# Two feed-forward layers: the first two weight pieces multiplied by token halves of 128 columns

## Chip, cores and metric

The kernel runs on one core of a Trainium2 chip. The metric is device time in microseconds (us) of one execution. Five engines work side by side: TensorE (PE; its weight loads are shown as PEld), VectorE (DVE), ScalarE (ACT), GpSimd (POOL) and SyncE (SP, which issues most transfers).

## What is computed

The program computes a hybrid attention layer with a 32-expert feed-forward part on 256 tokens of width 1024, and behind it a block of two layers. The change lies in that second block:

```python
for layer in range(DEPTH_2):
    h = rmsnorm(x, norm_mix_g[layer])
    ...
    x = x + y
    h = rmsnorm(x, norm_ffn_g[layer])
    x = x + swiglu_ffn(h, ffn_w_gate[layer], ffn_w_up[layer], ffn_w_down[layer])
return rmsnorm(x, final_g)
```

`swiglu_ffn` is `(silu(h @ w_gate) * (h @ w_up)) @ w_down`, with 256 rows in `h`, 1024 columns, and 2816 hidden columns. Layer 0 mixes tokens by Fourier and convolution heads ahead of it, layer 1 by a pooling mixer.

## The kernel before

Products of the feed-forward layers are made to nearly float32 precision out of three matmuls on rounded float32 (fp32r). Each weight matrix is cut into pieces of 128 hidden columns by 1024 rows. ScalarE rounds a piece to `wh` (L2527, function `hi`), VectorE subtracts that from the original to get `wl` (L1637, function `lo`), and the helper `mm3` (L573 to L576) multiplies high by high (L574), high by low (L575) and low by high (L576). The activations are held turned (features on partitions, tokens on columns), split in the same way into `HTH` and `HTL`, each [128, 8 groups `k` of features, 256 tokens]. So a piece takes 8 values of `k` times 3 = 24 matmuls, each with a weight load of 128x128 and 256 moving columns. Pieces `n` = 0 and 1 are the first two halves of the first gate unit, n = 2 and 3 those of the first up unit. Four pairs of buffers `wh`, `wl` go round: `hi` of piece n waits until piece n-4 is "used".

Each engine runs its own list of instructions strictly in the order in which the code writes it; semaphore counts with names (`done((...))`) tie the lists together. What leads into a feed-forward layer runs for two token halves `i` = 0 and 1 of 128 tokens:

1. PE ends the mixer's output matmuls (L1476 in layer 0, L1620 in layer 1) and VectorE adds them to the residual `X` (`add`, L2295), in two halves of 512 columns.
2. ScalarE sums the squares (`squares`, L2889) and takes the root (L2894), VectorE takes the reciprocal (L2299, in `scale`).
3. VectorE scales the half into `XN` (`normed`, L2310, two instructions).
4. PE turns it: 8 transposes of 128x128 (`turned`, L1393) into PSUM.
5. ScalarE writes the rounded `HTH` (`high`, L2907), VectorE the rest `HTL` (`low`, L2318), 8 instructions each of 128 columns. They go in groups `q`: half 0 has two groups of four values of `k`, half 1 has four groups of two.

On PE the order around it is: `turned(st, 0)`, then in `ffn` `turned(st, 1)`, then piece after piece over all 256 tokens; before the matmuls of piece 0 for k = 0, 2, 4, 6 `turned_ready` (L1396) waits for `HTL` of both halves:

```python
pe.wait_ge(*done(("HTL", l, 0, k // 4)))
pe.wait_ge(*done(("HTL", l, 1, k // 2)))
```

In layer 0 two of the mixer's last matmuls are kept behind `turned("ffn0", 0)`. In layer 1 ScalarE does `squares` of both halves ahead of `high`, and VectorE does `normed` of both halves ahead of `low`; `lo` of piece 1 stands behind all of `low`. POOL scales the pooling map (L3227 and L3232) long before layer 1 and then waits for the last mixer matmul.

The gate and up products of a step j fill two PSUM banks; behind them come the sigmoid, two multiplications, and the split into `FTH` and `FTL`; and after 44 pieces the 22 pieces of the down matrix. SyncE fetches weights into a ring of slots; `emptied` names the step that must be done before a slot is filled anew, for a gate unit the `lo` of its second piece.

Of the kernel before, what the change touches and what calls it, by code (L numbers as in the profile page):

```python
# [7 lines left out]
F32 = mybir.dt.float32  # L8
# [193 lines left out]
def build(nc, I, out, counts, counting):  # L202
    with ExitStack() as ctx:
# [23 lines left out]
        def done(name):  # L227

            if counting and name not in counts:
                return sig["pe_ada"].sem, 1  # L230
            key, n = counts[name]
            return sig[key].sem, n
# [316 lines left out]
        def emptied(name):  # L549

            kind = name[0]
            if kind in ("in", "out", "abc", "abr", "gate", "up", "down"):
                st, n = {
                    "in": lambda: ("in", AT_PIECE[name[1], 2 * name[2] + 1]),
                    "out": lambda: ("out", 2 * OUT_KK.index(name[1]) + 1),
                    "abc": lambda: ("ab", 2 * AB.index(name[1]) + 1),
                    "abr": lambda: ("ab", 9 + 2 * name[1]),
                    "gate": lambda: (f"ffn{name[1]}", 4 * name[2] + 1),
                    "up": lambda: (f"ffn{name[1]}", 4 * name[2] + 3),
                    "down": lambda: (f"ffn{name[1]}", 2 * NFF + 2 * name[2] + 1),  # L560
                }[kind]()
                return [(st, "lo", n)]
            if kind == "w1":
                return [("w1", name[1], name[2] + wide(name)), ("w1b", name[1], (0, 1, 2, 2)[name[2] // 2])]
            if kind == "w2":
                return [("w2", name[1], name[2] + wide(name)), ("w2b", name[1])]
            if kind == "dft":
                return [("width", 3)]
            if kind == "outab" and name[1] == 2:
                return [("outab", 3)]  # L570
            return [name]
# [15 lines left out]
        def _(pe):  # L587
# [801 lines left out]
            def turned(l, i):  # L1389
                for q, b, ks in turns(l, i):  # L1390
                    pe.wait_ge(*done(("normed", l, i, 0 if q == 0 else 1)))
                    for k in ks:
                        t = pe.transpose(turn_at(b, k, l, i), XN[:, i, k * 128:(k + 1) * 128], ident)  # L1393
                    t.then_inc(*P.tick(("n turned", l, i, q)))

            def turned_ready(l, k):  # L1396

                pe.wait_ge(*done(("HTL", l, 0, k // 4)))
                pe.wait_ge(*done(("HTL", l, 1, k // 2)))
# [149 lines left out]

            def ffn(l, then):  # L1550
                st, gu = f"ffn{l}", 4 - 4 * l
                turned(st, 1)
                for j in range(NFF // 2):
                    bg, bu = [(gu, gu + 1), (gu + 2, gu + 3)][j % 2]
                    for bank in (bg, bu):
                        for m in range(2):
                            n = 4 * j + 2 * (bank == bu) + m
                            _, hi, lo, _, _ = piece(st, n)
                            pe.wait_ge(*done((st, "lo", n)))
                            if bank == bg and m == 0 and j >= 2:  # L1560
                                pe.wait_ge(*done((st, "gated", j - 2)))
                            for k in range(8):
                                if n == 0 and k % 2 == 0:
                                    turned_ready(st, k)
                                t = mm3(pe, PS[:, bank, m * 256:(m + 1) * 256], hi[:, k, :], lo[:, k, :], HTH[:, k, :],
                                        HTL[:, k, :], k == 0, k == 7)
                            t.then_inc(*P.tick((st, "used", n)))

                def down(k, i, ns):
                    _, hi, lo, _, _ = piece(st, 2 * NFF + k)  # L1570
                    pe.wait_ge(*done((st, "lo", 2 * NFF + k)))
                    return mm3(pe, PS[:, 4 - gu + 2 * i + ns, :], FTH[:, k, i * 128:(i + 1) * 128],
                               FTL[:, k, i * 128:(i + 1) * 128], hi[:, ns * 512:(ns + 1) * 512],
                               lo[:, ns * 512:(ns + 1) * 512], k == 0, k == NFF - 1)

                for k in range(NFF - 4):
                    if k % 2 == 0:
                        pe.wait_ge(*done((st, "f", k // 2)))
                    for i, ns in LAST:
                        t = down(k, i, ns)  # L1580
                    t.then_inc(*P.tick((st, "used", 2 * NFF + k)))
                pe.wait_ge(*done((st, "f", NFF // 2 - 1)))
                for ks in ((NFF - 4, NFF - 3), (NFF - 2, NFF - 1)):
                    for ns in range(2):
                        for k in ks:
                            t = down(k, 0, ns)
                        if k == NFF - 1:
                            t.then_inc(*P.tick((st, "down", 0, ns)))
                for ns in range(2):
                    if ns:  # L1590
                        then()
                    for k in range(NFF - 4, NFF):
                        t = down(k, 1, ns)
                    t.then_inc(*P.tick((st, "down", 1, ns)))
# [36 lines left out]
        def _(dve):  # L1631
            V = sig["dve_ada"]

            def lo(st, n):
                src, h, l, _, _ = piece(st, n)
                dve.wait_ge(*done((st, "hi", n)))
                dve.tensor_tensor(l, src, h.bitcast(F32), ALU.subtract).then_inc(*V.tick((st, "lo", n)))  # L1637
# [664 lines left out]
            def base(l, i):  # L2302

                dve.wait_ge(*done(("sq", l, i)))
                dve.tensor_scalar(rb[i], sqs[i][0], 1.0 / 1024, 1e-6, ALU.mult, ALU.add).then_inc(*V.tick(("rb", l, i)))

            def normed(l, i):
                scale(l, i)
                for n, c in enumerate((slice(0, 256 << (1 - i)), slice(256 << (1 - i), 1024))):
                    dve.tensor_scalar(XN[:, i, c], X[:, i, c], rr[i], None, ALU.mult).then_inc(*V.tick(("normed", l, i, n)))  # L2310

            def low(l, i, qs):
                for q, b, ks in turns(l, i):
                    if q in qs:
                        dve.wait_ge(*done(("HTH", l, i, q)))
                        for k in ks:
                            c = slice(128 * i, 128 * i + 128)
                            t = dve.scalar_tensor_tensor(out=HTL[:, k, c], in0=turn_at(b, k, l, i),  # L2318
                                                         scalar=gk(GAIN[l])(k), in1=HTH[:, k, c].bitcast(F32),
                                                         op0=ALU.mult, op1=ALU.subtract)  # L2320
                        t.then_inc(*V.tick(("HTL", l, i, q)))
# [165 lines left out]
            normed("ffn1", 0)  # L2487
            add(1, 1, PS[:, 3, :], ("pmap",), "x5")
            base("ffn1", 1)
            normed("ffn1", 1)  # L2490
            low("ffn1", 0, [0])
            low("ffn1", 1, [0, 1])
            low("ffn1", 0, [1])
            low("ffn1", 1, [2, 3])
            lo("ffn1", 1)

            V = sig["dve_ffn1"]
            ffn(1, 2)
# [20 lines left out]
        def _(act):  # L2519
# [378 lines left out]
            def both(l, name, i):  # L2898
                for _ in squares(l, name, i):
                    pass  # L2900

            def high(l, i, qs):
                for q, b, ks in turns(l, i):
                    if q in qs:
                        act.wait_ge(*done(("n turned", l, i, q)))
                        for k in ks:
                            t = act.activation(HTH[:, k, 128 * i:128 * i + 128], turn_at(b, k, l, i), ACT.Copy,  # L2907
                                               scale=gk(GAIN[l])(k))
                        t.then_inc(*S.tick(("HTH", l, i, q)))
# [165 lines left out]
                               ACT.Copy).then_inc(*S.tick(("pooled", g)))  # L3075
            hi("ffn1", 1)
            both("ffn1", "x5", 0)
            both("ffn1", "x5", 1)
            high("ffn1", 0, [0])
            high("ffn1", 1, [0, 1])  # L3080
            high("ffn1", 0, [1])
            high("ffn1", 1, [2, 3])

            S = sig["act_ffn1"]
            ffn(1, 2)
# [10 lines left out]
        def _(pool):  # L3096
# [133 lines left out]
            for g in range(4):  # L3230
                for c in range(2):
                    pool.tensor_tensor(pm[:, g, c, :], pm[:, g, c, :], PSC[:, 256 * g:256 * g + 256], ALU.mult).then_inc(  # L3232
                        *G.tick("map scaled"))
            pool.wait_ge(*done(("pmap",)))
            small("final", FG, I["final_g_2"].rearrange("(a n) -> a n", a=1).to_broadcast([128, 1024]))

# [153 lines left out]
```

## Time and profile before

| what | us |
|---|---|
| median of three runs | 1626.15 (1625.92 to 1627.06) |
| the profiled execution's own time | 1627.0 |
| its span, first to last instruction | 1625.2 |
| PE busy | 1525.5 (94%) |
| VectorE busy | 670.8 (41%) |
| ScalarE busy | 456.1 (28%) |
| POOL busy | 111.4 (7%) |
| layer 0: first and 49th feed-forward matmul start | 1222.54 and 1229.05 |
| layer 1: first and 49th feed-forward matmul start | 1430.15 and 1438.50 |

The 49th matmul of a layer is the first of piece 2, so the stretch before it is that of pieces 0 and 1. The granted clock of TensorE is 1.00 at 2.4 GHz and 0.50 at 1.2 GHz. A matmul's busy time in the trace includes its way through the array, so neighbours overlap; the pace of a stream is read from the distance between starts.

### The profile page before, as it was taken

How to read it: one execution, taken by the hardware profiler on the slowest of the kernel's cores; microseconds unless marked ns; L12 is line 12 of the kernel's file. 1: busy time of each engine (PE TensorE's matmuls, PEld its weight loads, DVE VectorE, ACT ScalarE, POOL GpSimd, SP SyncE). 2: the span in 40 equal slices, each digit the busy share in tenths (PEclk: the TensorE clock that was granted, in tenths of full speed). 3: DMA queues.
4: the chain of work that ended last, by engine and by line, in shares of the span. 5: the costliest groups of instructions: out<-in, count | busy, mean ns of one | idle time of the engine just before them, and what ended most of it. 6: DMA issues, size and time to landing. Idle time of an engine off the chain costs nothing. (4 is left out here: it accounts for less than half of the span.)

```text
span 1625.2 us, 21576 instructions
## 1 busy us (share of the span) xinstructions
PE 1525.5 (94%) x8585; PEld 872.0 (54%) x8585; DVE 670.8 (41%) x970; ACT 456.1 (28%) x760; POOL 111.4 (7%) x124
## 2 busy tenths in 40 slices
PE   7999999999999998999998989887999999999998
PEld 4888534333333323333332323223849998799986
DVE  4676632323323222232222222224866655465654
ACT  3565311011101110111110101003765444354443
POOL 4132200000000000000000000000620003100000
PEclk9999999999999999999999989999999999999999
DMA  9977999999999999999999999999537555465530
GB/s 348 383 217 279 379 385 427 425 405 410 426 426 426 425 426 428 426 426 425 427 425 427 427 425 426 426 423 337 174 104 246 182 183 187 137 205 183 181 104 27
DMA packets 113394, 534.27 MB, mean 329 GB/s; under 512 B 7013, under 2 KB 70140, under 8 KB 87376
## 3 DMA queue, kind: packets, MB, share of 16 engines
q1 hardware_dynamic: 111232, 529.97, 82.2%
q8 instruction: 121, 1.98, 0.5%
q0 software_dynamic: 2000, 1.98, 0.4%
q14 instruction: 41, 0.34, 0.1%
HBM read 530.87 MB, written 1.05 MB: 327 GB/s over the span
## 5 line engine op out<-in xcount | busy, mean ns | idle before, releaser
L1019 PE MATMUL ps<-ring,arena 128*64 128x512 f32 x2024 | 485.2, 604 | 17.4 <-DMA ring<-in_w_mlp 15.3
L1019 PEld LDWEIGHTS ps<-ring,arena 128*64 128x64 f32 x2024 | 130.1, 136 | 252.6 <-issue 209.1
L1037 PE MATMUL ps<-ring,arena 128*64 128x512 f32 x1024 | 231.8, 598 | 19.4 <-DMA ring<-in_w_mlp 13.4
L1637 DVE TENSOR_TENSOR wl<-ring,wh 128x1024 fp32r<-128x1024 f32 x132 | 162.1, 1232 | 135.8 <-ACT wh L2527 135.8
L574 PE MATMUL ps<-hth,wh 128*128 128x256 f32 x704 | 201.1, 286 | 0.7 <-DVE htl L2318 0.7
L575 PE MATMUL ps<-htl,wh 128*128 128x256 f32 x704 | 198.9, 282 | 0.0
L576 PE MATMUL ps<-hth,wl 128*128 128x256 f32 x704 | 198.2, 282 | 0.0
L2118 DVE TENSOR_TENSOR arena<-ps,arena 128x1024 f32<-128x1024 f32 x68 | 83.3, 1224 | 249.4 <-PE ps L1044 244.0
L2527 ACT ACTIVATE wh<-ring 128x1024 fp32r<-128x1024 f32 x132 | 139.2, 1059 | 148.8 <-PE ps L576 148.7
L1037 PEld LDWEIGHTS ps<-ring,arena 128*64 128x64 f32 x1024 | 76.9, 137 | 166.8 <-issue 136.7
L2143 DVE TENSOR_TENSOR arena<-ps,arena 128x512 f32<-128x512 f32 x34 | 23.5, 691 | 337.5 <-PE ps L1037 334.4
L575 PEld LDWEIGHTS ps<-htl,wh 128*128 128x128 f32 x704 | 135.9, 193 | 0.0
L576 PEld LDWEIGHTS ps<-hth,wl 128*128 128x128 f32 x704 | 134.7, 191 | 0.0
L574 PEld LDWEIGHTS ps<-hth,wh 128*128 128x128 f32 x704 | 133.7, 190 | 1.2 <-issue 1.0
L2795 ACT ACTIVATE arena<-arena 128x512 f32<-128x512 f32 (+1 forms) x33 | 20.4, 617 | 303.3 <-DVE arena L2131 303.3
L2816 ACT ACTIVATE obh<-arena 128x512 fp32r<-128x512 f32 x30 | 18.9, 630 | 294.0 <-DVE arena L2143 294.0
L574 PE MATMUL ps<-wh,fth 128*128 128x512 f32 x176 | 69.7, 396 | 0.0
L575 PE MATMUL ps<-wl,fth 128*128 128x512 f32 x176 | 69.6, 395 | 0.0
L576 PE MATMUL ps<-wh,ftl 128*128 128x512 f32 x176 | 69.4, 395 | 0.0
L3211 POOL MEMSET arena<- 128x1144 f32 x1 | 1.1, 1063 | 951.0 <-DVE htl L2318 951.0
L2776 ACT ACTIVATE arena<-ps,arena 128x256 f32<-128x256 f32 x60 | 30.6, 559 | 117.9 <-PE ps L990 112.9
L574 PE MATMUL ps<-wp,ht 128*128 128x384 f32 (+1 forms) x128 | 46.2, 361 | 2.9 <-DVE wp L1637 2.7
(456 smaller groups left out, 1853.8 us busy)
## 6 DMA issues: line engine op xcount, KB each, us to landing
ring<-in_w_mlp SPq DMA_DIRECT2D x187, 2048.0 KB, 27.8
ring<-in_ffn_w_gate SPq DMA_DIRECT2D x22, 1024.0 KB, 5.4
ring<-in_ffn_w_up SPq DMA_DIRECT2D x22, 1024.0 KB, 5.4
ring<-in_ffn_w_down SPq DMA_DIRECT2D x22, 1024.0 KB, 4.9
ring<-in_w_ada SPq DMA_DIRECT2D x16, 1024.0 KB, 9.7
ring<-in_w_ada SPq DMA_DIRECT2D x16, 512.0 KB, 11.4
ring<-in_w_mlp SPq DMA_DIRECT2D x8, 1024.0 KB, 34.4
ring<-in_w_in SPq DMA_DIRECT2D x10, 768.0 KB, 12.6
```

The lines of the kernel that those rows point to most:

```text
L574: pe.matmul(o, lh, rh, start=first, stop=False)
L575: pe.matmul(o, lh, rl, start=False, stop=False)
L576: return pe.matmul(o, ll, rh, start=False, stop=last)
L1019: t = pe.matmul(PS[64 * g:64 * g + 64, HB[hb][ns], :], x[:, k8, :], u[:, f:f + 512], start=False, stop=k8 == 7)
L1037: t = pe.matmul(PS[64 * g:64 * g + 64, 3, :], a4[:, kc, 64 * kg:64 * kg + 64], u[:, c, g * 512:(g + 1) * 512], start=k8 == 0, stop=k8 == 7)
L1637: dve.tensor_tensor(l, src, h.bitcast(F32), ALU.subtract).then_inc(*V.tick((st, "lo", n)))
L2118: dve.tensor_tensor(x, PS[:, b:b + 2, :], x, ALU.add).then_inc(*tick(name))
L2143: dve.tensor_tensor(OBF, PS[:, bank, :], G2R, ALU.mult).then_inc(*tick(n_f))
L2527: act.activation(h, src, ACT.Copy).then_inc(*S.tick((st, "hi", n)))
L2776: act.activation(XGT[b % 2][:, k, :], PS[:, bank, (k % 2) * 256:(k % 2) * 256 + 256], ACT.Identity, scale=a2[:, k:k + 1], bias=sh2[:, k:k ...
L2795: act.activation(SIG[:, 0:n], GLU[:, 0:n], ACT.Sigmoid, scale=1.702).then_inc(*Q.tick(name))
L2816: act.activation(OBH[0], OBF, ACT.Copy).then_inc(*SM.same())
```

## The change

In both layers pieces 0 and 1 are multiplied over 128 tokens at a time. PE takes token half 0 for k = 0 to 3 of piece 0 and of piece 1 (24 matmuls of 128 moving columns), then turns half 1, then takes half 0 for k = 4 to 7 of both pieces (24), then half 1 of piece 0 and of piece 1 (48). From piece 2 on nothing changes. In layer 1 ScalarE and VectorE do their parts in another order, and POOL does the subtraction `lo` of piece 1, which waits for `hi` of that piece; SyncE's wait for the slot of layer 1's first gate unit names both pieces, since two engines now read it.

```diff
@@ def emptied(name)
+            if name == ("gate", 1, 0):
+                return [("ffn1", "lo", 0), ("ffn1", "lo", 1)]
@@ block.tensor, def ffn(l, then)
                 st, gu = f"ffn{l}", 4 - 4 * l
-                turned(st, 1)
+
+                def token_half(n, i, k):
+                    _, hi, lo, _, _ = piece(st, n)
+                    c, o = slice(128 * i, 128 * i + 128), n * 256 + 128 * i
+                    return mm3(pe, PS[:, gu, o:o + 128], hi[:, k, :], lo[:, k, :], HTH[:, k, c], HTL[:, k, c],
+                               (n, i, k) == (0, 0, 0), (n, i, k) == (1, 1, 7))
+
+                for q in range(2):
+                    pe.wait_ge(*done(("HTL", st, 0, q)))
+                    for n in range(2):
+                        pe.wait_ge(*done((st, "lo", n)))
+                        for k in range(4 * q, 4 * q + 4):
+                            token_half(n, 0, k)
+                    if q == 0:
+                        turned(st, 1)
+                for n in range(2):
+                    for k in range(8):
+                        if k % 2 == 0:
+                            pe.wait_ge(*done(("HTL", st, 1, k // 2)))
+                        t = token_half(n, 1, k)
+                    t.then_inc(*P.tick((st, "used", n)))
                 for j in range(NFF // 2):
                     bg, bu = [(gu, gu + 1), (gu + 2, gu + 3)][j % 2]
-                    for bank in (bg, bu):
+                    for bank in (bg, bu) if j else (bu,):
@@
                             for k in range(8):
-                                if n == 0 and k % 2 == 0:
-                                    turned_ready(st, k)
@@ block.vector
             base("ffn1", 1)
+            low("ffn1", 0, [0])
             normed("ffn1", 1)
-            low("ffn1", 0, [0])
-            low("ffn1", 1, [0, 1])
             low("ffn1", 0, [1])
-            low("ffn1", 1, [2, 3])
-            lo("ffn1", 1)
+            low("ffn1", 1, range(4))
@@ block.scalar
             both("ffn1", "x5", 0)
-            both("ffn1", "x5", 1)
+            part = squares("ffn1", "x5", 1)
+            next(part)
             high("ffn1", 0, [0])
-            high("ffn1", 1, [0, 1])
+            next(part)
             high("ffn1", 0, [1])
-            high("ffn1", 1, [2, 3])
+            high("ffn1", 1, range(4))
@@ block.gpsimd
+            src, high, low, _, _ = piece("ffn1", 1)
+            pool.wait_ge(*done(("ffn1", "hi", 1)))
+            pool.tensor_tensor(low, src, high.bitcast(F32), ALU.subtract).then_inc(*G.tick(("ffn1", "lo", 1)))
```

The change adds lines above these places, so L574 to L576 of before are L576 to L578 of the changed program, L1393 is L1395, L1476 is L1478.

On PE at the start of layer 0's feed-forward part the order before is this (L1393 the transposes; `wh_91` and `wl_92` belong to piece 0):

```order
L1393 MATMUL ps<-arena 128x128 x8
L1476 MATMUL ps<-ring,arena 128x512 x2
L1393 MATMUL ps<-arena 128x128 x8
L574 MATMUL ps<-hth,wh_91 128x256
L575 MATMUL ps<-htl,wh_91 128x256
L576 MATMUL ps<-hth,wl_92 128x256
L574 MATMUL ps<-hth,wh_91 128x256
```

In the changed program the same place reads as follows (L1395 the transposes; `wh_93` and `wl_94` belong to piece 1; 18 more matmuls of 128 columns stand where the rows are left out):

```order
L1478 MATMUL ps<-ring,arena 128x512 x2
L576 MATMUL ps<-hth,wh_91 128x128
L577 MATMUL ps<-htl,wh_91 128x128
L578 MATMUL ps<-hth,wl_92 128x128
...
L576 MATMUL ps<-hth,wh_93 128x128
L577 MATMUL ps<-htl,wh_93 128x128
L578 MATMUL ps<-hth,wl_94 128x128
L1395 MATMUL ps<-arena 128x128 x8
L576 MATMUL ps<-hth,wh_91 128x128
```

The second turning has moved from ahead of all feed-forward matmuls to behind the first 24 of them, and these have 128 columns. In layer 1 the two turnings, which stood together, are parted in the same way.

On VectorE the order ahead of layer 1's feed-forward part is this before (L2295 `add`, L2310 `normed`, L2318 `low`, L1637 `lo`):

```order
L2295 TENSOR_TENSOR arena<-arena,ps 128x512
L2305 TENSOR_SCALAR arena<-arena 128x1
L2299 RECIPROCAL arena<-arena 128x1
L2310 TENSOR_SCALAR arena<-arena 128x256
L2310 TENSOR_SCALAR arena<-arena 128x768
L2318 SCALAR_TENSOR_TENSOR htl<-ps,arena,hth 128x128 x16
L1637 TENSOR_TENSOR wl_94<-ring,wh_93 128x1024
```

and this in the changed program (L2338 is `low`, L2330 `normed`, L2319 the reciprocal):

```order
L2315 TENSOR_TENSOR arena<-arena,ps 128x512
L2325 TENSOR_SCALAR arena<-arena 128x1
L2338 SCALAR_TENSOR_TENSOR htl<-ps,arena,hth 128x128 x4
L2319 RECIPROCAL arena<-arena 128x1
L2330 TENSOR_SCALAR arena<-arena 128x256
L2330 TENSOR_SCALAR arena<-arena 128x768
L2338 SCALAR_TENSOR_TENSOR htl<-ps,arena,hth 128x128 x12
L1657 TENSOR_TENSOR wl_96<-ring,wh_95 128x1024
```

Four instructions of `low` stand ahead of the second half's reciprocal and scaling, and piece 1's subtraction has gone to POOL.

## Rows read from the trace of the kernel before

**Rows 1.** The page: busy time of each engine, and granted clock in 40 slices.

```profile
PE 1525.5 (94%) x8585; PEld 872.0 (54%) x8585; DVE 670.8 (41%) x970; ACT 456.1 (28%) x760; POOL 111.4 (7%) x124
...
PEclk9999999999999999999999989999999999999999
```

**Rows 2.** Stretches: stretch, length, busy us (count) of each engine, granted clock, DMA share, GB/s.

```profile
1218.00:1220.60 2.60, 0.00 (x0) 0.00 (x0) 2.49 (x10) 1.18 (x4) 0.59 (x1) 1.00 0.55 126
1220.60:1222.50 1.90, 1.84 (x8) 1.34 (x8) 1.09 (x3) 1.26 (x5) 0.00 (x0) 0.57 1.12 396
1230.00:1400.00 170.00, 170.00 (x1224) 159.94 (x1223) 96.15 (x93) 76.34 (x84) 18.45 (x16) 1.00 0.59 192
...
1427.90:1430.10 2.20, 1.43 (x8) 0.84 (x8) 2.20 (x8) 2.11 (x9) 0.00 (x0) 0.77 1.10 388
1430.10:1435.00 4.90, 4.84 (x23) 4.88 (x24) 4.78 (x13) 3.43 (x8) 0.00 (x0) 0.50 0.27 103
```

**Rows 3.** Timeline into layer 0: start, us, engine, instruction, [idle before, releaser].

```profile
1215.10 1.04 PE L1393 MATMUL ps<-arena 128*128 128x128 f32 x8
...
1217.17 1.13 DVE L2318 SCALAR_TENSOR_TENSOR htl<-ps,arena,hth 128x128 fp32r<-128x128 f32 x4 [0.87 <-ACT hth L2907]
...
1220.20 0.88 DVE L2310 TENSOR_SCALAR arena<-arena 128x256 f32<-128x256 f32 x2
...
1220.61 2.07 PE L1393 MATMUL ps<-arena 128*128 128x128 f32 x8 [2.75 <-DVE arena L2310]
...
1222.54 0.55 PE L574 MATMUL ps<-hth,wh 128*128 128x256 f32 x1
...
1224.46 0.28 PE L574 MATMUL ps<-hth,wh 128*128 128x256 f32 x1
...
1229.05 0.28 PE L574 MATMUL ps<-hth,wh 128*128 128x256 f32 x1
```

**Rows 4.** Timeline into layer 1.

```profile
1418.66 1.05 ACT L2527 ACTIVATE wh<-ring 128x1024 fp32r<-128x1024 f32 x1
...
1425.34 1.04 PE L1393 MATMUL ps<-arena 128*128 128x128 f32 x8
...
1427.95 1.53 PE L1393 MATMUL ps<-arena 128*128 128x128 f32 x8 [1.57 <-DVE arena L2310]
...
1430.15 0.55 PE L574 MATMUL ps<-hth,wh 128*128 128x256 f32 x1 [0.68 <-DVE htl L2318]
...
1435.84 0.33 PE L576 MATMUL ps<-hth,wl 128*128 128x256 f32 x1
...
1438.50 0.28 PE L574 MATMUL ps<-hth,wh 128*128 128x256 f32 x1
```

**Rows 5.** Timeline of PE: float32 matmuls of 128 and of 64 moving columns.

```profile
73.39 2.84 PE L719 MATMUL ps<-arena 128*128 128x128 f32 x24
...
122.10 0.39 PE L743 MATMUL ps<-arena 128*128 128x64 f32 x2
122.33 0.39 PE L744 MATMUL ps<-arena 128*128 128x64 f32 x2
```

**Rows 6.** Instructions that read or write hth, and L745's: duration ns minimum/median/maximum.

```profile
L574 PEld LDWEIGHTS ps<-hth,wh x704: 186/187/330, 1222.5 to 1557.4; 128*128 128x128 f32 x176
...
L745 PEld LDWEIGHTS ps<-arena x24: 192/192/193, 121.8 to 140.7; 128*128 128x128 f32 x24
```

**Rows 7.** Timeline of PE: fp32r matmuls of 512 moving columns, in layer 0's down part.

```profile
1411.15 0.40 PE L575 MATMUL ps<-wl,fth 128*128 128x512 f32 x1
...
1412.55 0.40 PE L575 MATMUL ps<-wl,fth 128*128 128x512 f32 x1
```

**Rows 8.** Timeline of PE into the first mixer (1130 to 1136 us).

```profile
1130.23 3.67 PE L1393 MATMUL ps<-arena 128*128 128x128 f32 x16 [3.84 <-DVE arena L2310]
...
1135.58 0.28 PE L576 MATMUL ps<-hth,wm 128*128 128x256 f32 x1
```

**Rows 9.** POOL's timeline ahead of layer 1.

```profile
1377.91 8.47 POOL L3232 TENSOR_TENSOR ring<-ring,arena 128x256 f32<-128x256 f32 x8
```

## The prediction

> **What bounds the kernel now.** I read the page first. TensorE is busy for 94% of the span, no other engine for half of it, and the granted clock is nearly always full [rows 1]. The stretches show the same for the feed-forward layers: from 1230 to 1400 us TensorE is busy in every microsecond and moves no more than the matmuls need, while VectorE, ScalarE and the transfers have time to spare [rows 2]. So whatever the change wins or loses before piece 2 of a layer goes straight to the end of the program. The two places to look at are the ways into the layers, and for those I read the timelines.
>
> Layer 0: TensorE turns half 0 at 1215.10, VectorE has finished the first group of its `HTL` at 1217.17 + 1.13 = 1218.30, but TensorE does nothing for 2.6 us [rows 2], waits for the second half's scaling, turns it from 1220.61, and begins piece 0 at 1222.54. Piece 2 begins at 1229.05 [rows 3]. The idle time costs twice: in the stretch 1220.60 to 1222.50 the clock is granted at 0.57 on average, that is mostly at 1.2 GHz [rows 2], and only from about 1224.3 on are the matmuls at full pace: 39 from 1224.46 to 1229.05, 0.118 us apart [rows 3]. Layer 1: half 0 is turned from 1425.34, half 1 from 1427.95, piece 0 begins at 1430.15; the clock is at 0.50 from 1430.10 to 1435.00 [rows 2], 27 matmuls from 1430.15 to 1435.84 start 0.211 apart, then the clock is full, and piece 2 begins at 1438.50 [rows 4].
>
> **The price that decides: a matmul of 128 columns.** The change makes 96 matmuls of 128 columns in each layer out of 48 of 256. The columns are the same, the weight loads are doubled. No row shows an fp32r matmul with 128 moving columns, so I bound it.
> - From below: 512 columns start 0.233 apart (six from 1411.15 to 1412.55) [rows 7], 256 columns 0.118 [rows 3]. That is 0.00045 us a column, and 128 columns would take 0.0605 us, if the weight load never showed.
> - From above, as one instruction: not more than 256 columns take, 0.118 us.
> - The nearest rows: float32 matmuls with the same 128x128 weights. 24 with 128 columns take 2.84 us with the last one's 0.28 in it, so 23 steps of 0.111. And pairs with only 64 columns take 122.33 - 122.10 = 0.23, so 0.111 to 0.115 each again [rows 5]. Half the columns, the same pace: what sets it is not the columns but the weight load. The load of an fp32r matmul lasts 187 ns in the trace, that of those float32 ones 192 [rows 6], so I take it to be the same load.
>
> I take 0.111 us, from these rows. Ninety-six then cost 10.66 us, where 48 of 256 columns cost 5.66 at full clock: the halves save nothing on the array and double the loads. The Trainium skill has two rules here, and they disagree. In "TensorE: Matmul & The Clock Gate", section "Back-to-back issue gap", the isolated gap is columns/2.4 + 2.5 ns, which is 56 ns for 128 columns and would make the change a gain; its section "LDWEIGHTS (loading the stationary operand)" gives weight columns/1.2 ns, 107 ns for 128, and [rows 5] agree with that one.
>
> **Layer 0, step by step.** The first 24 matmuls can start when the first group of `HTL` is there, at 1218.30, say 1218.4 (4.1 us sooner than now). The clock is still granted in full from 1218.00 to 1220.60 [rows 2], although TensorE rests there; with matmuls in that stretch I take it to stay so. 24 x 0.111 = 2.66, to 1221.06. The second half's scaling runs from 1220.20 to 1221.08 [rows 3], so the transposes, which now stand behind the 24, find it ready and begin 0.45 us later than now; at full clock 8 take 0.89 (the first eight took 1.04 including the last one's way through [rows 3]), to 1221.95. While ScalarE and VectorE make the second half's `HTH` and `HTL`, TensorE has the next 24 matmuls of half 0, to 1224.6. By then these eight copies and subtractions, 2.4 us long now, are done, so nothing waits. 72 x 0.111 = 7.99, to 1229.94. Against 1229.05: **+0.9 us**.
>
> **Layer 1.** From the turning's start to the first group of `HTL` layer 0 takes 1218.30 - 1215.10 = 3.2 us [rows 3]; ScalarE and VectorE now do this group first here too, so it is ready at 1425.34 + 3.2 = 1428.5, and TensorE starts at 1428.6, 1.55 us sooner. TensorE idles for 2.2 us ahead of that. The clock fell at about 1429.1 in the present run after 1.6 us of idle (0.77 over 1427.90 to 1430.10 is 1.2 us at full and 1.0 at half [rows 2]), and I expect it to fall there again. It then stays low for 3.4 us, as in layer 0 (from about 1220.9, read off 0.57 over its stretch, to 1224.3), or twice that, as here now (1429.1 to 1435.9). I take the short one, since matmuls now run through without a gap. At half clock a matmul with 128x128 weights starts every 0.213 to 0.22 us (transposes: 16 in 3.67 [rows 8]). So 4.5 matmuls by 1429.1, 16 by 1432.5, 3.5 to 1432.9. The scaling of half 1, which now lets the transposes go at 1427.95 [rows 4], slides behind one group of copies and subtractions, by about 1.1 us. That costs nothing, because the transposes must wait for TensorE until 1432.9 anyway: this is what is late next. Transposes to 1433.8, 72 matmuls to 1441.8. Against 1438.50: **+3.3 us**.
>
> **The rest.** `lo` of piece 1 on POOL: 8 of 256 columns take 8.47 us [rows 9], so 1024 take 4.2 us, from the end of `hi` of piece 1 at 1418.66 + 1.05 = 1419.7 [rows 4] to 1424; it is wanted at 1429. Cover: 5 us. If it slowed VectorE in that time, some tenths would be lost in adds that TensorE's mixer matmuls hide. VectorE is freed of 1.2 us. ScalarE and VectorE prepare pieces 2 and 3 (four instructions, about 4.5 us in a chain) behind the second half's groups, in layer 1 by about 1439; they are wanted at 1441.8. SyncE's wait for the slot of the first gate unit now has two names, and the later one is met some 10 us sooner than now: nothing. PSUM: the bank written early is free, its adds are long done.
>
> **Sum.** +0.9 and +3.3 are +4.2 us on a span of 1625.2. The profiled execution took 1627.0, 0.85 above the median; the difference is the same for both, so 1626.15 + 4.2 = **1630.3 us**. A measurement can tell about 0.2%, 3.25 us, from no change: this is just beyond it.
>
> **Rivals.**
> 1. *No low clock in layer 1.* With matmuls from 1428.6 the clock may not fall at all. Then layer 1 loses 1.65 instead of 3.3, together +2.5: 1628.7, no change to measure. Against it: 2.2 us of idle stand ahead. Chance 0.17.
> 2. *Faster: the weight load hides under 128 columns.* At the lower bound of 0.0605 us TensorE reaches the transposes of layer 0 before 1220.61, waits for the scaling, ends them at 1221.8 and 72 matmuls at 1226.2: -2.9. Layer 1: 24 to 1431.0 (0.12 at low clock), transposes to 1432.7, 72 to 1437.1: -1.4. Together -4.3: 1621.9. It decides at the price of a matmul: 192 of them at 0.088 us are even, below 0.070 the change is faster by over 0.2%. For it: the turning of half 1 is truly hidden. Against it: 64 columns went no faster than 128 [rows 5]. The 56 ns of the Trainium skill's "Back-to-back issue gap" would be this case; the same section has 81 ns for a sustained stream of loads and matmuls, which would give about -1 us; no row shows either. Chance 0.11.
> 3. *Short fp32r matmuls go at the plain float32 rate.* A plain float32 product shows as two matmul records of 0.111 us each [rows 5]. Were 128 columns of fp32r treated so, 192 more records make +21.3: 1651.6. For it: no fp32r matmul below 256 columns is in the kernel. Chance 0.06.
> 4. *The short matmuls hold the clock low.* If a stream that is half weight loads doesn't bring the clock back, 72 matmuls and more at 0.213 give +10.8 and +13.3: 1650.3. Against it: before the first mixer the clock came back at 1135.5 after 16 transposes of 128 columns, a gap and five matmuls [rows 8]. Chance 0.06.
>
> **How the numbers follow.** The forecast has 0.60: of that 0.50 lies above +3.25 and 0.10 below it (a pace of 0.105 already takes 1.2 us off). Rival 1 gives 0.17 to no change; rival 2 has 0.09 for faster and 0.02 for no change; rivals 3 and 4 give 0.12 to slower. Sum: faster 0.09, no change 0.29, slower 0.62. Range: on the upper side a short low clock in layer 0 too (+1.6), the long one in layer 1 (+1.6) and 0.118 for the pace (+1.3) reach 1635; on the lower side it takes in rival 1 and the upper half of rival 2, to 1623.5. Rivals 3 and 4 and the rest of 2 are left out, about 0.2.
>
> **What would show it.** Right: 128-column matmuls 0.111 us apart at full clock; the first at about 3.2 us behind the first turning; no idle time between them, and transposes of half 1 waiting for TensorE, not for VectorE; piece 2 at about +0.9 us in layer 0 and +4.2 in layer 1 against now. Wrong: starts 0.06 to 0.09 apart, or 0.22 at full clock; a clock that stays at 0.50 beyond four microseconds; TensorE waiting for the second half's `HTL`, or for piece 1 from POOL.

## The result, and the profile after

The changed kernel takes 1632.97 us in the median of six runs (1631.65 to 1635.96), the kernel before 1626.04 (1624.36 to 1627.06). The ratio is 1.0045 with a 95% interval of 1.0034 to 1.0056: 6.9 us slower, where 4.2 were forecast. The profiled execution took 1635.96 us, the slowest of the six, with a span of 1634.2.

The page of the changed kernel, lines that answer to [rows 1]:

```profile
PE 1538.0 (94%) x8681; PEld 881.2 (54%) x8681; DVE 669.9 (41%) x969; ACT 456.1 (28%) x760; POOL 113.4 (7%) x125
...
PEclk9999999999999999999999999998999999999999
```

TensorE has 96 more matmuls (8681 against 8585) and is busy 12.5 us longer. Where the time went is read by stretches, each from one start to another in the same trace, so that a later beginning doesn't count. The timeline of PE into layer 0 (start, us, engine, instruction, [idle before, releaser]), against [rows 3]:

```profile
1216.68 1.04 PE L1395 MATMUL ps<-arena 128*128 128x128 f32 x8
...
1219.92 0.33 PE L576 MATMUL ps<-hth,wh 128*128 128x128 f32 x1 [0.49 <-DVE htl L2338]
...
1222.66 1.06 PE L1395 MATMUL ps<-arena 128*128 128x128 f32 x8
1223.47 0.31 PE L576 MATMUL ps<-hth,wh 128*128 128x128 f32 x1
1223.62 0.28 PE L577 MATMUL ps<-htl,wh 128*128 128x128 f32 x1
1223.73 0.27 PE L578 MATMUL ps<-hth,wl 128*128 128x128 f32 x1
...
1231.55 0.33 PE L576 MATMUL ps<-hth,wh 128*128 128x256 f32 x1
```

The half matmuls start 0.11 us apart; 72 of them and the step to the next take 1231.55 - 1223.47 = 8.08 us, 0.112 each. The transposes wait for TensorE and for nobody else. From the first turning to piece 2: 14.87 us, before 13.95.

Into layer 1, against [rows 4], all engines:

```profile
1429.54 1.04 PE L1395 MATMUL ps<-arena 128*128 128x128 f32 x8
...
1432.53 0.33 PE L576 MATMUL ps<-hth,wh 128*128 128x128 f32 x1 [1.95 <-DVE htl L2338]
...
1433.14 0.40 PE L578 MATMUL ps<-hth,wl 128*128 128x128 f32 x1
1433.33 0.42 PE L576 MATMUL ps<-hth,wh 128*128 128x128 f32 x1
1433.55 0.41 PE L577 MATMUL ps<-htl,wh 128*128 128x128 f32 x1
...
1437.18 1.93 PE L1395 MATMUL ps<-arena 128*128 128x128 f32 x8
1437.86 2.17 ACT L2925 ACTIVATE hth<-ps,arena 128x128 fp32r<-128x128 f32 x8 [4.58 <-PE ps L1395]
...
1439.86 0.34 PE L578 MATMUL ps<-hth,wl 128*128 128x128 f32 x1
1440.04 0.28 PE L576 MATMUL ps<-hth,wh 128*128 128x128 f32 x1
...
1447.40 0.34 PE L576 MATMUL ps<-hth,wh 128*128 128x256 f32 x1
```

The clock falls within the half matmuls, at 1433.15, from then on they start 0.21 us apart, and it is full again only at 1439.97, 6.8 us later. ScalarE waits 4.58 us for the second turning, which is queued behind the 24 halves. From the first turning to piece 2: 17.86 us, before 13.16.

The stretches of the changed kernel (stretch, length, busy us and count of PE, PEld, DVE, ACT, POOL, granted clock, DMA share, GB/s), against [rows 2]:

```profile
1219.90:1231.50 11.60, 11.57 (x104) 11.58 (x105) 8.39 (x19) 6.15 (x14) 0.42 (x1) 1.00 0.97 316
1415.00:1418.00 3.00, 1.40 (x7) 0.79 (x5) 0.75 (x2) 0.80 (x3) 0.00 (x0) 1.00 0.00 0
1418.00:1421.00 3.00, 2.00 (x11) 2.00 (x12) 2.11 (x4) 1.75 (x3) 0.00 (x0) 0.75 0.00 0
1429.50:1432.50 3.00, 1.07 (x9) 0.79 (x7) 2.09 (x8) 2.29 (x9) 0.62 (x1) 1.00 0.42 122
1432.50:1440.00 7.50, 7.47 (x38) 7.47 (x39) 3.44 (x13) 2.92 (x13) 0.00 (x0) 0.54 0.88 303
1440.00:1447.40 7.40, 7.40 (x68) 7.40 (x68) 4.27 (x6) 2.98 (x4) 0.00 (x0) 1.00 0.37 117
```

Layer 0 has a full clock throughout, layer 1 a low one for 6.8 of the 7.5 us. And there is a third place that was not in the forecast: the pooling stage, where the clock is low too, from 1419.5 to 1422.9. The second group of pooling matmuls is that place's row in both timelines, first before, then changed:

```profile
1416.47 2.12 PE L1604 MATMUL ps<-ring,arena 128*128 128x136 f32 x16 [2.60 <-DVE ring L2469]
```

```profile
1419.00 3.56 PE L1624 MATMUL ps<-ring,arena 128*128 128x136 f32 x16 [2.60 <-DVE ring L2489]
```

The same 2.60 us of rest ahead of it, the same work, 1.4 us longer. The sum of the two profiled spans, 1634.2 - 1625.2 = 9.0 us:

| stretch | before | changed | difference |
|---|---|---|---|
| start to layer 0's first turning | 1215.10 | 1216.68 | +1.58 |
| layer 0, first turning to piece 2 | 13.95 | 14.87 | +0.92 |
| piece 2 to layer 1's first turning | 196.29 | 197.99 | +1.70 |
| layer 1, first turning to piece 2 | 13.16 | 17.86 | +4.70 |
| piece 2 to the end | 186.70 | 186.80 | +0.10 |

The first line lies ahead of everything that the change touches. All traces below differ there (the first turning of layer 0 is at 1212.4 to 1216.7). The timed runs of one kernel scatter by about as much; that it is for the same reason is not shown, since only one or two runs of each kernel have a trace.

### The profile page after: what moved, and what is told of

Its sections match the earlier page's. It is cut to its first block and busy times, and to the rows that moved or that the text cites. A ratio compares the mean times of both kernels' runs of the same rounds, so it can differ in the third digit from the quotient of the medians.

```text
span 1634.2 us, 21765 instructions
## 1 busy us (share of the span) xinstructions
PE 1538.0 (94%) x8681; PEld 881.2 (54%) x8681; DVE 669.9 (41%) x969; ACT 456.1 (28%) x760; POOL 113.4 (7%) x125
## 5 line engine op out<-in xcount | busy, mean ns | idle before, releaser
L576 PE MATMUL ps<-hth,wh 128*128 128x256 f32 (+1 forms) x736 | 209.2, 284 | 2.4 <-DVE htl L2338 2.4
L577 PE MATMUL ps<-htl,wh 128*128 128x256 f32 (+1 forms) x736 | 207.0, 281 | 0.0
L578 PE MATMUL ps<-hth,wl 128*128 128x256 f32 (+1 forms) x736 | 206.5, 281 | 0.0
L577 PEld LDWEIGHTS ps<-htl,wh 128*128 128x128 f32 x736 | 141.5, 192 | 0.0
L576 PEld LDWEIGHTS ps<-hth,wh 128*128 128x128 f32 x736 | 139.4, 189 | 3.5 <-DVE htl L2338 3.5
L578 PEld LDWEIGHTS ps<-hth,wl 128*128 128x128 f32 x736 | 140.5, 191 | 0.0
L576 PE MATMUL ps<-wh,fth 128*128 128x512 f32 x176 | 69.7, 396 | 0.0
L578 PE MATMUL ps<-wh,ftl 128*128 128x512 f32 x176 | 69.4, 394 | 0.0
L576 PE MATMUL ps<-wp,ht 128*128 128x384 f32 (+1 forms) x128 | 46.1, 360 | 2.9 <-DVE wp L1657 2.7
```

Of the source, the lines that this page charges most:

```text
L576: pe.matmul(o, lh, rh, start=first, stop=False)
L577: pe.matmul(o, lh, rl, start=False, stop=False)
L578: return pe.matmul(o, ll, rh, start=False, stop=last)
```

## The experiments

The verdicts rest on two measures: the ratio of the timed runs, which resolves 1 to 2 us here, and the same two stretches in each trace, which resolve a tenth within one execution but move with the clock from one execution to the next. "L0" and "L1" are the times from a layer's first turning to piece 2; before they are 13.95 and 13.16, changed 14.87 and 17.86.

### One layer at a time

For layer 0 alone, the halves stand under a condition, and layer 1 runs as before:

```diff
-                turned(st, 1)
+                if l == 0:
+                    def token_half(n, i, k):
...
+                else:
+                    turned(st, 1)
```

> Layer 0 in token halves, layer 1 as before. Theory (doubled weight loads against an earlier start, two layers that add up): piece 2 of layer 0 begins 14.9 us behind the first turning instead of 13.95, so +0.9 us in the median, and the way into layer 1 is that of before (13.2 us from turning to piece 2). Rival (the loss sits in layer 0's halves and what they set off later, the clock of the pooling stage among it): +2.5 us or more.

Measured: 1627.62 against 1627.23 us, ratio 1.0001 (0.9990 to 1.0011). L0 14.88, L1 11.72. The +0.93 of layer 0 is that of the changed kernel; the timed runs can't tell it from nothing, but they exclude the rival's +2.5. L1 was expected at 13.2 and came out at 11.72, in code that is that of before: the low clock there varies from one execution to the next.

For layer 1 alone, the condition is turned round, and the orders of the change on ScalarE, VectorE and POOL are kept.

> Layer 1 in token halves with the new order on ScalarE, VectorE and POOL, layer 0 as before. Theory: +4.7 us as in the changed kernel's trace if the low clock lasts 6.7 us, +3.3 if it lasts 3.4; the median between 3.3 and 5. Rival (the loss of the changed kernel is spread): +3 or less.

Measured: 1633.24 us, ratio 1.0036 (1.0023 to 1.0049), 5.9 us by the ratio and above the 3.3 to 5 expected. L0 14.25, L1 24.18. So layer 1 carries the loss, and in the profiled execution, the slowest of the six with 1641.43 us, it was 11 us, not 4.7. L0 is code of before, and 14.25 where the trace of before has 13.95: the low clock there began 0.9 us behind the second turning, at 1222.86, in place of 0.3, and ended at 1226.27. The clock stayed low through all halves (columns as above):

```profile
1433.00:1436.00 3.00, 3.00 (x16) 3.00 (x16) 0.47 (x2) 1.13 (x5) 0.00 (x0) 0.50 1.03 354
1436.00:1440.00 4.00, 4.00 (x21) 4.00 (x21) 3.67 (x9) 2.94 (x7) 0.00 (x0) 0.50 0.04 13
1440.00:1445.00 5.00, 5.00 (x26) 5.00 (x25) 0.38 (x1) 0.00 (x0) 0.00 (x0) 0.50 0.64 208
1445.00:1450.00 5.00, 5.00 (x25) 5.00 (x25) 1.23 (x1) 1.06 (x1) 0.00 (x0) 0.50 0.01 5
```

TensorE is busy in every microsecond and its clock doesn't come back.

### The price of the halves without their place

Both halves are turned first, in the order of before; only pieces 0 and 1 are multiplied as 96 matmuls of 128 columns.

```diff
                 turned(st, 1)
+                for n in range(2):
+                    pe.wait_ge(*done((st, "lo", n)))
+                    for k in range(8):
+                        if n == 0 and k % 2 == 0:
+                            turned_ready(st, k)
+                        for i in range(2):
+                            t = token_half(n, i, k)
+                    t.then_inc(*P.tick((st, "used", n)))
...
```

> Order of before in both layers, all halves turned first; only the 48 matmuls of pieces 0 and 1 are made as 96 of 128 columns. Theory (the weight load sets the pace): 0.111 us apart at full clock, so 96 x 0.111 - 48 x 0.118 = +5.0 us in each layer, +10 in all; at low clock each costs 0.213 like one of 256 columns, so the first 9 and 27 slots hold half the work and the sum is rather +11 to +13. Rival (the 128-column matmul costs half and the loss came from the order): within 1 us of before.

Measured: 1655.7 us, ratio 1.0179 (1.0165 to 1.0193): +28.5 us. L0 27.91, L1 25.34. Both theories miss. The trace of layer 0 shows why (stretch, then the end of the halves in the timeline):

```profile
1222.70:1243.20 20.50, 20.50 (x98) 20.50 (x97) 5.23 (x9) 3.95 (x7) 0.00 (x0) 0.50 0.54 176
```

```profile
1242.77 0.41 PE L575 MATMUL ps<-htl,wh 128*128 128x128 f32 x1
1242.98 0.41 PE L576 MATMUL ps<-hth,wl 128*128 128x128 f32 x1
1243.19 0.52 PE L574 MATMUL ps<-hth,wh 128*128 128x256 f32 x1
...
1245.01 0.38 PE L576 MATMUL ps<-hth,wl 128*128 128x256 f32 x1
1245.22 0.28 PE L574 MATMUL ps<-hth,wh 128*128 128x256 f32 x1
```

All 96 halves, 20.5 us, run at the low clock that the rest ahead of them left. 2.0 us into the matmuls of 256 columns it is full again. Before, the same place was low for 3.4 us. All five timed runs lie at 1653.4 us or above. This is the mechanism of rival 4, for which I had 0.06.

I then formed the theory that a stream of halves doesn't raise a low clock but holds a full one. The same kernel with idle matmuls on TensorE's rests tests it; `fill` is the tool of all runs below with idle matmuls:

```diff
+                def fill(times, cols=256):
+                    _, hi, _, _, _ = piece(st, 0)
+                    pe.wait_ge(*done((st, "lo", 0)))
+                    for _ in range(times):
+                        pe.matmul(PS[:, gu + 1, 0:cols], hi[:, 0, :], hi[:, 0:2, :].rearrange("p k n -> p (k n)")[:, 0:cols],
+                                  start=True, stop=True)
+
+                fill(22 if l == 0 else 12)
                 turned(st, 1)
+                fill(4)
```

> Halves behind both turnings in both layers, as in the run that was 28 us slower, with the same idle matmuls as the run before this one. Theory (a stream of 128-column matmuls does not bring a low clock back, but holds a full one): every half matmul 0.111 us apart at full clock, so 5.0 us a layer more than 48 of 256 columns; in all +7 us against before, +10 against before with idle matmuls. Rival (such a stream lowers the clock by itself): low clock again and +20 or more.

Measured: 1633.52 us, ratio 1.0049 (1.0034 to 1.0063): +6.9 us against before, as expected; against before with idle matmuls (1625.71, below) 7.8 where 10 was expected. L0 18.14, L1 15.57. All halves at full clock:

```profile
1221.70:1232.50 10.80, 10.79 (x98) 10.79 (x97) 5.04 (x9) 3.76 (x7) 0.00 (x0) 1.00 1.03 343
```

### The changed kernel with its rest in layer 1 filled

```diff
+                fill(0 if l == 0 else 15)
                 for q in range(2):
                     pe.wait_ge(*done(("HTL", st, 0, q)))
```

> The changed kernel with 15 more matmuls of 256 columns into an unused bank on TensorE in layer 1, between the first turning and the wait for its HTL. Theory (two thirds of layer 1's loss is the low clock that the 2 us of rest bring): the clock stays full there, 24 halves in 2.7 us, and the kernel is 3 us faster than the changed one (from +6.9 to about +3.9 against before); the first half matmul starts at the same place or at most 0.2 us later. Rival (the clock is not set by that rest): no change against the changed kernel, low clock in the same place.

Measured: 1629.68 us, ratio 1.0016 (1.0007 to 1.0026): against the kernel before beside it (1627.23) a loss of 2.5 us in place of 6.9. L0 14.88, L1 14.61 in place of 17.86. The first half starts 2.99 us behind the turning, as without idle matmuls. Timeline and stretches:

```profile
1427.35 1.04 PE L1395 MATMUL ps<-arena 128*128 128x128 f32 x8
1428.14 2.04 PE L1565 MATMUL ps<-wh 128*128 128x256 f32 x15
1430.34 0.33 PE L576 MATMUL ps<-hth,wh 128*128 128x128 f32 x1 [0.16 <-DVE htl L2346]
```

```profile
1427.30:1430.30 3.00, 2.88 (x24) 2.63 (x23) 2.10 (x8) 2.28 (x9) 0.62 (x1) 1.00 0.51 121
1430.30:1442.00 11.70, 11.66 (x105) 11.66 (x105) 7.73 (x18) 5.93 (x15) 0.00 (x0) 1.00 0.70 231
```

So the low clock was 3.25 us of layer 1's 4.70. The other 1.45 are against a layer that had 6.8 us of low clock itself. Against the kernel before with its rests filled (L0 13.18, L1 11.61, below) the change costs 1.70 us in layer 0 and 3.00 in layer 1 at full clock, and the traces split that in two:

| us | layer 0 | layer 1 |
|---|---|---|
| price of the halves at full clock: late halves with idle matmuls, less before with them | 18.14 - 13.18 = +4.96 | 15.57 - 11.61 = +3.96 |
| the early start (in layer 1 with the new orders): this run, less late halves with idle matmuls | 14.88 - 18.14 = -3.26 | 14.61 - 15.57 = -0.96 |
| together, at full clock | +1.70 | +3.00 |
| lost to the low clock before | 13.95 - 13.18 = 0.77 | 13.16 - 11.61 = 1.55 |
| lost to it in the changed kernel's profile | 0 | 17.86 - 14.61 = 3.25 |

With these, 1.70 - 0.77 = +0.93 and 3.00 + 3.25 - 1.55 = +4.70 are the two differences of the profiles. The price is 1 us lower in layer 1, where 256 columns at full clock have to stop for an `HTL` (0.61 us, shown below) and the halves don't. The idle time that the change removes was worth less than the doubled matmuls even where no clock fell.

### The changed kernel once more

> The changed kernel once more, for a second trace. Theory (layer 1's loss depends on where the low clock meets the half matmuls): layer 0 again 14.9 us from turning to piece 2; layer 1 one of three values, about 14.8 (no low clock), 17.9 (low for the first halves) or 24 (low through all halves, as in the run with layer 1 alone). Rival (layer 1's loss is fixed): 17.9 again.

Measured: a single run of 1641.94 us. L0 14.87, L1 23.99. The stretch of the halves in layer 1:

```profile
1430.50:1451.50 21.00, 21.00 (x105) 21.00 (x105) 7.68 (x18) 5.87 (x14) 0.00 (x0) 0.53 0.47 158
```

The same program, the same rest (1.96 us of waiting against 1.95), and the clock low for 7 us in one execution, and in the other from about the 12th half to the last and beyond. The two are not equally common: this stream of layer 1 was run 13 times (six runs of the changed kernel, this one, six with layer 1 alone), and two lie above 1641 us, this one and the profiled one of the run with layer 1 alone. The other eleven took 1631.5 to 1636.0 us.

### The kernel before with its rests filled

> The kernel before, with idle matmuls of 256 columns (into an unused bank) on TensorE while it rests: layer 0, 22 ahead of the second turning and 4 behind it; layer 1, 12 and 4. Nothing else is moved. Theory (half of what the changed kernel does well is only the clock): the clock is full at both ways in, layer 0 from turning to piece 2 takes 13.0 us instead of 13.95 and layer 1 10.4 instead of 11.7 to 13.2, so 2 to 3.5 us faster than before. Rival (the clock falls for other reasons, or the idle matmuls push the real ones back): no gain, or a loss of up to 1 us.

Measured: 1625.71 against 1626.58 us, ratio 0.9993 (0.9983 to 1.0003). L0 13.18, L1 11.61, at full clock. The traces show the 2.3 us (0.77 and 1.55) that were expected at the lower end, although L1 was expected at 10.4; the timed runs can't tell them from nothing, and layer 1 of before has 11.7 to 13.2 anyway.

> The kernel before with the same number of idle matmuls, of 64 moving columns each, weights 128x128 as ever. Theory (the weight load sets the pace): they too start 0.111 us apart, like those of 128 columns, so they fill the rest as well; whether they hold the clock is open. Rival (columns set the pace, 128 columns cost 0.111 for another reason): 0.06 apart or less.

The edit is the 64 as second argument of `fill`. Measured: 1622.78 us, ratio 0.9984 (0.9972 to 0.9997). L0 13.13, L1 11.58. The first of the 22 idle matmuls of layer 0 begins while the last mixer matmul of 512 columns still runs, so the pace is read from the 20 behind the first two (timeline of PE from 1215.5 and from 1218.0). First the row with 64 columns, then that of the run with 256:

```profile
1215.29 2.40 PE L1556 MATMUL ps<-wh 128*128 128x64 f32 x20
```

```profile
1217.75 2.55 PE L1556 MATMUL ps<-wh 128*128 128x256 f32 x20
```

With the last one's 0.28 us taken off, 19 steps of 0.112 and of 0.119 us. A quarter of the columns saves 6% of the time: the theory holds in its size too, and the rival (0.06 or less) falls. Matmuls of 64 columns held the full clock as well.

That it is the weights, and not a fixed price of any matmul, the trace of before shows. Float32 matmuls of a single moving column, first with weights of 128 columns, then of 64:

```profile
1181.58 1.05 PE L1496 MATMUL ps<-arena 128*128 128x1 f32 x8
```

```profile
195.17 1.10 PE L997 MATMUL ps<-arena,st 128*64 128x1 f32 x32
```

With the last one's 0.25 and 0.20 us taken off, the steps are 0.114 and 0.029 us. The narrow ones fill half of the output's partitions each and start in pairs, every 0.058 us; so a matmul as such has no price of 0.11, and the pace goes with the width of the weights.

> The kernel before with idle matmuls at four rests: the two of the feed-forward layers as above, 18 of 256 columns in the pooling stage ahead of its second matmul group, and 4 products of 384 float32 columns ahead of the first mixer's turning. Theory: the low clock from 1128.7 to 1135.5 goes as well, which costs 16 transposes and 5 matmuls about 0.1 us each, so 2 us more than the two rests alone: 4 to 5.5 us faster than before. Rival: the first mixer's way in is bound by ScalarE and VectorE, and the clock there is worth nothing: same as the two rests.

The two further places:

```diff
             P = sig["pe_pool"]
+            _, last_hi, _, _, _ = piece("ffn0", 3 * NFF - 1)
+            pe.wait_ge(*done(("x4", 0, 1)))
+            for _ in range(18):
+                pe.matmul(PS[:, 0, 0:256], last_hi[:, 0:128], last_hi[:, 0:256], start=True, stop=True)
             pool_over(1)
...
+            pe.wait_ge(*done(("x2", 0, 0)))
+            for _ in range(4):
+                pe.matmul(PS[:, 2, 0:384], ident, CT(C_IE, 384), start=True, stop=True)
             turned("mix0", 0)
```

Measured: 1624.84 us, ratio 0.9992 (0.9983 to 1.0001). L0 13.17, L1 11.59. From the first mixer's turning to that of layer 0 it takes 84.14 us in place of 84.87, so the full clock there (0.96 from 1128 to 1135) is worth 0.7 us and not 2, and the 4 to 5.5 us expected in all were not reached. That this way in is mostly bound by ScalarE and VectorE is the likely reason, not a shown one. The pooling stage kept its clock (196.27 us between the layers), as it did in six other traces without idle matmuls in that place.

### The new order on ScalarE, VectorE and POOL by itself

Layer 1 with 256 columns and the change's orders, at full clock:

> 256 columns in both layers; in layer 1 the change's order on ScalarE, VectorE and POOL (first group of half 0 ahead of the second half's scaling, lo of piece 1 on POOL), with idle matmuls of 256 columns (22 and 4 in both layers), so at full clock. Theory: without halves the new order only makes half 1 later, by one group of copies and subtractions: layer 1 from turning to piece 2 takes 12.5 to 13 us against 11.6 with the old order and idle matmuls. Rival (the order is good by itself): 11.6 or less.

Measured: 1625.69 us, ratio 0.9998 (0.9988 to 1.0008). L0 13.19, L1 11.41 where I expected 12.5 to 13. My theory for it falls: the first matmul does start 0.8 us later (5.63 us behind the turning in place of 4.82), but then nothing interrupts the stream. With the old order and a full clock PE waits for `HTL` ahead of the first matmul and once more within the stream, where the 13th starts 0.89 us behind the 12th (timeline of PE, kernel before with rests filled):

```profile
1429.18 0.36 PE L574 MATMUL ps<-hth,wh 128*128 128x256 f32 x1 [0.34 <-DVE htl L2327]
1431.46 0.35 PE L574 MATMUL ps<-hth,wh 128*128 128x256 f32 x1 [0.61 <-DVE htl L2327]
```

The new order costs nothing and gains nothing: the next run, with the old order and only the subtraction on POOL, has the same 11.41.

> The kernel with idle matmuls at four rests, and of the change only piece 1's lo on POOL in layer 1. Theory: VectorE's lo of piece 1 ended some tenths after TensorE wanted it at full clock; layer 1 from turning to piece 2 11.2 us against 11.6, and in all 3 to 5 us faster than before. Rival (POOL slows VectorE): 11.6 or more.

The edit is the POOL part of the change alone, with VectorE's `lo("ffn1", 1)` removed and the four rests filled. Measured: 1624.5 against 1626.89 us, ratio 0.9988 (0.9978 to 0.9998). L0 13.19, L1 11.41, 0.2 less than without: with VectorE's `lo` piece 1 started some 0.2 us late, with POOL's it doesn't. The kernel is faster than before by 2.4 us by the medians (0.3 to 3.6 by the interval), where 3 to 5 were expected; how much of that is the subtraction the timed runs can't tell. The idle matmuls ahead of the first mixer did not keep the clock in this trace: it was low from 1134.43 to 1137.84, and from the first mixer's turning to layer 0's it took 85.92 us.

## Why the prediction was right, and where it was not

**The price of a half matmul** was the step that decided the sign, and it was right: 0.111 to 0.112 us at full clock, against bounds of 0.0605 and 0.118. What had been read from float32 rows held for fp32r. Two kernels that differ only in halves (rests filled in both) give 18.14 - 13.18 = 4.96 us in layer 0 where 96 x 0.111 - 48 x 0.118 = 5.0 was worked out, and weights of 64 columns go faster where fewer moving columns don't, which bears out the reason given, the weight load. The Trainium skill's 107 ns for a weight load of 128 columns ("TensorE: Matmul & The Clock Gate", section "LDWEIGHTS (loading the stationary operand)") agrees with these rows, its 56 ns gap and its 81 ns for a sustained stream ("Back-to-back issue gap") don't: no stream with 128x128 weights that was read here went below the 0.109 us of the transposes.

**Layer 0**: forecast +0.9, measured +0.92 and in three more traces +0.93, +0.92 and +0.93. Full clock, transposes behind the 24 halves, no waits: as written. That it came out to 0.02 us is in part luck, since all these are against one trace of before: the same code took 14.25 us in the run with layer 1 alone, against which the change loses 0.6.

**Layer 1**: forecast +3.3, measured +4.70, and +10.8 in the second trace. The step that failed is "It then stays low for 3.4 us ... I take the short one, since matmuls now run through without a gap." It was the long one, 6.8 us, or the whole stream, and with it came the prediction's own sign of being wrong, a clock at 0.50 beyond four microseconds. That a stream without gaps is enough was the mistake: in four of five places TensorE was busy with matmuls of 128 columns and 128x128 weights and the clock stayed low to their end. A second weakness is the base: layer 1 of before took 13.16 us in the trace that the forecast used and 11.72 in the run with layer 0 alone, so the loss depends by 1.4 us on which execution it is counted from. Of the reason given against rival 4, the 16 transposes, a gap and five matmuls at 1130 to 1135.5 [rows 8], the five matmuls had 256 columns, and I read them as if the transposes had done it. Rival 4 as priced (both layers low, +24) didn't happen, since layer 0 starts at full clock; in layer 1 it happens in some executions. It deserved more than 0.06, with the price of one layer. That price was too high as well: a clock low from 1429.1 on gives by the prediction's own steps 91.5 x 0.213 + 8 x 0.22 = 21.25 us, so +11.9 and not +13.3, and +10.8 was measured.

**The first half's start** came 2.99 us behind the turning in layer 1, forecast 3.2: on the safe side.

**The rest**: POOL's subtraction of 1024 columns took 2.36 us where 4.2 had been scaled from other operations; its cover was never needed. Nobody waited for SyncE. Not in the forecast was the pooling stage, +1.70 in the profiled execution; it came in four of the five traces with the change's new orders and idle matmuls nowhere in that stage (not in that of layer 1 alone), and in one of the six that keep the orders of before (the run with both halves turned first, where the same pooling matmuls take 2.71 us in place of 2.12). Whether the new orders favour it or it is chance was not settled.

**The median**: +6.9 against +4.2. In the profiled execution the layers lose 5.6 us and the pooling stage 1.7, together 7.3. Executions in which layer 1 loses 11 us are not in the median: all six runs of the changed kernel took 1635.96 us or less, and the profiled one, with 4.70 in layer 1, is the slowest of them. The other five have no trace, so how their 6 to 7 us are made up is not shown. The forecast of slower held, in the range of 1623.5 to 1635.0, with layer 1 mis-sized by 1.4 us and the pooling stage missing.

## What to carry to other kernels

Cutting the moving side of a matmul in two saves nothing when its weight load takes as long as the whole matmul did: compare the pace of a stream with a row of the same weights and fewer columns before using halves to start early. A rest of two microseconds can cost twice (the one of 2.60 us in the pooling stage did so in five of eleven traces), and in these runs what followed it decided how long: 48 matmuls of 256 columns or 96 of 128 behind the same rest differed by 28.5 us in two layers, and by 7.8 with the rests filled in both kernels. So a stream of small matmuls behind a rest is worth a look at the granted clock, and idle matmuls ahead of it are a cheap test. And where a low clock appears in one execution and not in the next, look at several traces before pricing it.

## What the runs showed that I had not expected

A continuous stream of fp32r matmuls of 128 columns stayed at 1.2 GHz for 20.5 us with TensorE busy in all of it, and in four of the five places where such a stream met a low clock in a trace, the clock stayed low to its end and beyond (L0 27.91 and L1 25.34 in one kernel, L1 24.18 and 23.99 in two others). These are the four stretches of low clock, two with all halves turned first, then layer 1 alone, then the changed kernel's second trace:

```profile
1221.32:1245.21 23.89, 23.89 (x111) 23.70 (x112) 6.46 (x12) 6.24 (x12) 0.00 (x0) 0.50 0.53 173
1446.60:1470.49 23.89, 23.55 (x110) 23.59 (x111) 8.72 (x16) 5.83 (x12) 0.00 (x0) 0.50 0.35 113
1431.07:1454.96 23.89, 23.89 (x115) 23.89 (x114) 7.85 (x16) 6.18 (x12) 0.00 (x0) 0.50 0.36 122
1431.80:1455.69 23.89, 23.89 (x115) 23.89 (x114) 7.64 (x15) 6.18 (x12) 0.00 (x0) 0.50 0.36 119
```

All four are of one length, 23.9 us, and end 2.0 to 4.2 us after the last half, with matmuls of 256 columns running by then. In the kernel before, where 256 columns follow the rest directly, the low clock lasted 3.4 us in layer 0 and 6.8 in layer 1, and in layer 1 the last 5.8 us of it were filled with these matmuls. That the halves keep the clock low, and the 256 columns end it, fits all of this; since the four streams of halves were almost equally long, no run here separates it from a low clock of that one length, and a longer stream of halves would.

The same stream at full clock held it for 10.8 us, and idle matmuls of 64 columns held it through a rest of 2.7 us. In the fifth place, the changed kernel's own profile, the clock came back within the halves, a microsecond behind eight transposes; in another execution of the same program and in the run with layer 1 alone, with the transposes in the same place of the stream, it did not. What decides between them is open. By their times, eleven of thirteen executions with transposes within the halves were like the milder one, and none of the five with all transposes ahead of them.
